# Down projections of four feed-forward blocks computed as seven products of quarters in two passes, with sums of weight quarters made in DRAM by adding transfers

## What is computed

```
u = x @ w_up                       # x: 512 x 1024, w_up and w_gate: 1024 x 2816
g = causal_dwconv(x @ w_gate, ...) # second block: no convolution
down = (silu(g) * u) @ w_down      # w_down: 2816 x 1024
```

## Time and profile before

| | us |
|---|---|
| median of 3 runs (2281.48 to 2284.59) | 2281.77 |
| span of the profiled execution | 2280.9 |
| TensorE busy | 2245.4 (98%) |
| VectorE busy | 1367.0 (60%) |
| ScalarE busy | 1072.6 (47%) |
| GpSimd busy | 737.0 (32%) |
| DMA | mean 98 GB/s |

### The profile page before, as it was taken

One profiled execution on the slowest core, in us unless ns is written; L12 is line 12 of the kernel. 1 busy time (PEld: TensorE's weight loads), 2 busy tenths in 40 slices (PEclk: granted clock), 3 DMA queues, 4 the chain that ended last, 5 costly groups with the idle time before them and its releaser, 6 DMA issues.

```text
span 2280.9 us, 36680 instructions
## 1 busy us (share of the span) xinstructions
PE 2245.4 (98%) x13358; PEld 1934.1 (85%) x13358; DVE 1367.0 (60%) x1963; ACT 1072.6 (47%) x1850; POOL 737.0 (32%) x334
## 2 busy tenths in 40 slices
PE   8999999999999999999999999999999999999998
PEld 6668899988888887899988899988878768999987
DVE  7967666660453436666631899950557963899811
ACT  6665444442555554344432544441535665444512
POOL 6944422244322325321344311144111003311252
PEclk9999999999999999999999999999999999999999
DMA  6632332232211133223332233332422002323332
GB/s 211 197 93 94 110 107 98 99 101 96 80 65 66 64 103 120 96 98 101 102 100 85 93 102 110 95 106 95 149 82 75 29 11 83 107 98 109 101 102 93
DMA packets 64432, 223.79 MB, mean 98 GB/s; under 512 B 7120, under 2 KB 7120, under 8 KB 64336
## 3 DMA queue, kind: packets, MB, share of 16 engines
q1 hardware_dynamic: 60192, 208.30, 27.9%
q10 hardware_dynamic: 4144, 14.16, 2.0%
HBM read 211.88 MB, written 2.10 MB: 94 GB/s over the span
## 4 chain that ended last, share of the span: by engine, by line
PE 86%; DVE 5%; ACT 4%; issue 3%; DMA 1%; POOL 1%; DVEq 0%; SPq 0%; ACTq 0%; POOLq 0%
PE banks L645 9%; PE banks L678 9%; PE banks L680 9%; PE banks L679 9%; PE banks L646 9%; PE banks L647 9%; PE banks L859 5%; PE banks L860 5%; PE banks L861 5%; PE banks L906 3%; PE banks L905 3%; PE banks L904 3%; DVE banks L2603 2%; DMA raw<-ws 1%; PE banks L1257 1%
## 5 line engine op out<-in xcount | busy, mean ns | idle before, releaser
L563 POOL TENSOR_TENSOR wL<-raw,wH 128x1024 fp32r<-128x1024 f32 x194 | 497.6, 2570 | 756.9 <-ACT wH L1457 756.7
L1457 ACT ACTIVATE wH<-raw 128x1024 fp32r<-128x1024 f32 x371 | 391.9, 1058 | 680.8 <-PE banks L680 393.8
L645 PE MATMUL banks<-xH,wH 128*128 128x512 f32 (+1 forms) x1080 | 413.3, 383 | 11.2 <-DVE xL L2135 7.2
L646 PE MATMUL banks<-xL,wH 128*128 128x512 f32 (+1 forms) x1080 | 407.7, 377 | 0.0
L647 PE MATMUL banks<-xH,wL 128*128 128x512 f32 (+1 forms) x1080 | 407.5, 377 | 0.0
L678 PE MATMUL banks<-wH,hH 128*128 128x512 f32 x704 | 273.9, 389 | 0.0
L679 PE MATMUL banks<-wH,hL 128*128 128x512 f32 x704 | 273.9, 389 | 0.0
L680 PE MATMUL banks<-wL,hH 128*128 128x512 f32 x704 | 273.9, 389 | 0.0
L645 PEld LDWEIGHTS banks<-xH,wH 128*128 128x128 f32 x1080 | 203.6, 189 | 56.6 <-DVE wL L2140 7.9
L647 PEld LDWEIGHTS banks<-xH,wL 128*128 128x128 f32 x1080 | 203.6, 189 | 38.1
L646 PEld LDWEIGHTS banks<-xL,wH 128*128 128x128 f32 x1080 | 203.8, 189 | 35.1
(11 more groups left out here) (381 smaller groups left out, 5229.3 us busy)
## 6 DMA issues: line engine op xcount, KB each, us to landing
raw<-ws SPq DMA_DIRECT2D x371, 512.0 KB, 3.3
shifted<-gpad SPq DMA_DIRECT2D x32, 258.0 KB, 4.9
w1b<-w ACTq DMA_DIRECT2D x8, 512.0 KB, 5.6
tmp<-rows ACTq DMA_DIRECT2D x7, 512.0 KB, 3.8
b_row<-rows ACTq DMA_DIRECT2D x5, 512.0 KB, 3.8
tmp<-xT SPq DMA_DIRECT2D x8, 256.0 KB, 6.0
xr<-xN ACTq DMA_DIRECT2D x4, 512.0 KB, 3.7
out<-xr SPq DMA_DIRECT2D x3, 512.0 KB, 2.7
```

Source lines behind the costliest of these rows:

```text
L563: pool.tensor_tensor(wL[:, j, :], raw[:, j, :], fp(wH[:, j, :]), ALU.subtract).then_inc(low_ready, 1)
L645: pe.matmul(bank, wH[:, slot, cols], rh, start=start, stop=False)
L646: pe.matmul(bank, wH[:, slot, cols], rl, start=False, stop=False)
L1457: act.activation(wH[:, c % SLOTS, :], raw[:, c % SLOTS, :], ACT.Copy).then_inc(high_ready, 1)
```

## The change

A down projection is the product of a 512 x 2816 matrix h and a 2816 x 1024 matrix w. The change cuts tokens, hidden channels (11 chunks each) and output columns in halves and computes the four output quarters from seven products of 256 x 1408 by 1408 x 512, in Winograd's arrangement. Each product takes 2 token tiles x 11 chunks x 3 matmuls of 512 columns.

- Pass one makes products 1, 5, 6 and 4 over 11 pairs of chunks, each into 2 banks; ScalarE copies all eight banks into `tmp` (`keep_part`), and GpSimd joins them to three tiles (`down_parts`: fifth - first, sixth - first, first + fourth).
- Pass two makes products 2 and 3, into the banks 4 to 7 of the second half of the tokens (VectorE adds the kept sixth in `seed_banks`), and product 7 into the banks 0 and 2 of the first half. These are completed from the kept tiles: in parts 0 and 1 by adding the kept tiles to the residual ahead (`add_kept`), in parts 2 and 3 by `join_block`, two VectorE operations for each of the two token tiles of the first half, before `post_block` and `update_block` can have them.
- The weights of a down projection now are 39 chunks: 22 chunks of quarters and their sums (DRAM tensor `sums`), 11 plain ones (`X_AT`) and 6 with a third kind of sum (`thirds`, `Y_AT`). GpSimd makes these sums in DRAM with transfers: 14 plain copies of up to 1 MB for each down projection (`copy_base`: for part 0 beside the chunks of the second pointwise projection and the first gate `ple0`, for 1 and 2 beside those of the first attention, for 3 in the second attention), and, beside gate and up, for each of 11 pairs four transfers of 256 KB that add to their destination: the first and the third together, then the second, which waits for the first, and the fourth, which waits for the second. The next pair waits for the fourth and the third.
- The down chunks go through two rings of four slots: the second ring lies where `xH` and `xL` (the parts of x) are, so it can be filled once gate and up are over. Their low parts are VectorE's. The first four chunks of the following stage are all loaded when 36 of the 39 chunks are used up.
- The parts of h are formed pair by pair (`part_sums`, `parts_high`, `part_lows`) in rings of four in `mixXH` and `mixXL`; `hH` and `hL` are gone.
- Semaphores of the row loads are merged to make room for the new ones.

The diff, cut to its core:

```diff
+NP = FT // 2
+X_AT = [FT + 3 * (k // 2) + k % 2 for k in range(9)] + [FT + 15, FT + 16]
+Y_AT = [FT + 3 * (k // 2) + 2 for k in range(8)] + [FT + 13, FT + 13, FT + 14]
...
+DOWN = FT + NP + len(Y_CHUNKS)
...
+            def load_down(inst):
+
+                d0 = CHUNK[f"down{inst}"]
+                for i in range(DOWN):
+                    c = d0 + i
+                    if i < SLOTS:
+                        sp_e.wait_ge(chunk_done, c - SLOTS + 1)
+                    else:
+                        sp_e.wait_ge(chunk_done, max(d0, c - 2 * SLOTS + 1))
+                    to = raw_slot(c)
+                    if i < FT:
+                        sp_e.wait_ge(sum_added, 16 * (3 * (NP * inst + i // 2) + (3 if i % 2 else 1)))
+                        sp_e.dma_start(to, sums[FT * inst + i]).then_inc(loaded(c), 16)
+                    elif i in Y_STARTS:
+                        a, b = Y_CHUNKS[Y_STARTS.index(i)]
+                        w = (b - a + 1) * S
+                        sp_e.wait_ge(third_added, 16 * (NP * inst + b + 1))
+                        sp_e.dma_start(to[:, 0:w], thirds[inst, :, a * S:a * S + w]).then_inc(loaded(c), 16)
+                    else:
+                        sp_e.dma_start(to, ws[c]).then_inc(loaded(c), 16)
+                if inst < 3:
+                    for c in range(d0 + DOWN, d0 + DOWN + SLOTS):
+                        sp_e.wait_ge(chunk_done, d0 + DOWN - SLOTS + 1)
+                        sp_e.dma_start(raw[:, c % SLOTS, :], ws[c]).then_inc(raw_loaded[c % SLOTS], 16)
...
                         low_of_last_sum(u, 1, t)
+                        second_sum(inst, 0, t)
                         low_of_last_sum(u, 2, t)
+                        fourth_sum(inst, 0, t)
+                    first_and_third(inst, SEVENS[inst] - 1)
                     low_of_last_sum(u, 1, SEVENS[inst] - 1)
-                    d0 = CHUNK[f"down{inst}"]
-                    for i in (d0, d0 + 1):
-                        split(i // SLOTS, i % SLOTS)
-                    return d0 + 2
...
+            def copy_base(inst, n):
+
+                d0 = CHUNK[f"down{inst}"]
+                if n < NP:
+                    to, src = FT * inst + 2 * n, d0 + 2 * n
+                    pool.dma_start(sums[to:to + 2].rearrange("c p n -> (c p) n"),
+                                   ws[src:src + 2].rearrange("c p n -> (c p) n")).then_inc(bases_copied, 16)
...
+            def first_and_third(inst, j, t=0):
+
+                c, d = FT * inst + 2 * j, CHUNK[f"down{inst}"] + 2 * j
+                if NP * inst + j:
+                    pool.wait_ge(sum_added, t * 48 + 48 * (NP * inst + j))
+                    pool.wait_ge(third_added, t * 16 + 16 * (NP * inst + j))
+                    pool.sem_inc(adding, 1)
+                pool.dma_start(half_of(sums, t * 2 + c, 1), half_of(ws, t * 2 + d, 0), accum_op=ALU.add).then_inc(sum_added, 16)
+                pool.dma_start(thirds[inst, :, bass.ds(t * S + j * S, S)], half_of(ws, t * 2 + (d + 1), 1), accum_op=ALU.add)\
+                    .then_inc(third_added, 16)
...
+            def second_sum(inst, j, t=0):
+
+                c = FT * inst + 2 * j
+                pool.wait_ge(sum_added, t * 48 + 48 * (NP * inst + j) + 16)
+                pool.sem_inc(adding, 1)
+                pool.dma_start(half_of(sums, t * 2 + (c + 1), 1), half_of(sums, t * 2 + c, 1), accum_op=ALU.add)\
+                    .then_inc(sum_added, 16)
...
-                def h_there(k):
-                    pe.wait_ge(h_ready, FT * inst + k + 1)
-                full_product(f"down{inst}", FT, hH, hL, h_there, banks_free)
+                d0 = CHUNK[f"down{inst}"]
+                lows, parts = DOWN * inst, A_PARTS * inst
+
+                def product(bank, g, n, t, i, half, start=False):
+
+                    a, w = slice(t * P, t * P + P), slice(half * S, half * S + S)
+                    high, low = mixXH[:, g % 4, n, a], mixXL[:, g % 4, n, a]
+                    w_high, w_low = high_slot(d0 + i)[:, w], low_slot_of(d0 + i)[:, w]
+                    pe.matmul(ps[bank], high, w_high, start=start, stop=False, skip_group_check=True)
+                    pe.matmul(ps[bank], low, w_high, start=False, stop=False, skip_group_check=True)
+                    return pe.matmul(ps[bank], high, w_low, start=False, stop=False, skip_group_check=True)
...
+                def second_and_third(k, t, seed=False):
+                    pe.wait_ge(a_low, parts + 3 * NP + 2 * k + 2)
+                    pe.wait_ge(down_low, lows + X_AT[k] + 1)
+                    product(4 + 2 * t, NP + k, 2, t, X_AT[k], 0)
+                    if seed:
+                        pe.wait_ge(seeded, 2 * inst + t + 1)
+                    return product(5 + 2 * t, NP + k, 1, t, X_AT[k], 1)
+
+                def seventh(k, t):
+                    pe.wait_ge(a_low, parts + 3 * NP + 2 * k + 2)
+                    pe.wait_ge(down_low, lows + Y_AT[k] + 1)
+                    return product(2 * t, NP + k, 0, t, Y_AT[k], k % 2)
+
+                pe.sem_inc(low_ready, DOWN)
...
+                    sixth_and_fourth(j).then_inc(chunk_done, 1)
+                first_and_fifth(NP - 2).then_inc(chunk_done, 1)
+                first_and_fifth(NP - 1).then_inc(part_done, 1)
+                sixth_and_fourth(NP - 2).then_inc(chunk_done, 1)
+                sixth_and_fourth(NP - 1).then_inc(chunk_done, 2)
+
+                pe.wait_ge(part_kept, 8 * inst + 4)
+                for k in range(0, NP - 3, 2):
+                    for x in (k, k + 1):
+                        second_and_third(x, 0, seed=x == 4)
+                        second_and_third(x, 1, seed=x == 4).then_inc(chunk_done, 1)
...
+                        pe.wait_ge(part_kept, 8 * inst + 6)
+                    for y in (k, k + 1):
+                        seventh(y, 0)
+                        mm = seventh(y, 1)
+                    mm.then_inc(chunk_done, 1)
+                second_and_third(NP - 3, 0)
+                second_and_third(NP - 3, 1).then_inc(chunk_done, 1)
+                for y in (NP - 3, NP - 2):
+                    seventh(y, 0)
+                    mm = seventh(y, 1)
+                mm.then_inc(chunk_done, 1)
+                seventh(NP - 1, 0).then_inc(block_done, 1)
+                seventh(NP - 1, 1).then_inc(block_done, 1)
+                second_and_third(NP - 2, 0).then_inc(chunk_done, 1)
+                second_and_third(NP - 1, 0).then_inc(block_done, 1)
+                second_and_third(NP - 2, 1)
+                second_and_third(NP - 1, 1).then_inc(chunk_done, 2)
 
...
+                if q < 2 and name != "wout":
+                    act.wait_ge(whole_made, 2 * (2 * int(name == "down3") + q) + 2)
+                elif q < QT - 1:
...
+                def keep_part(to, bank, n):
+                    if n < 4:
+                        act.wait_ge(part_done, 3 * inst + n)
...
-                        low_h(0)
+                        part_sums(0)
+                        low_of_chunk(1)
                     dve.wait_ge(product_done, t * 5 + (5 * u + 5))
                     dve.tensor_tensor(gate, half_bank(4), w, ALU.subtract).then_inc(seven_sum, 1)
                     if inst < 2:
                         older_taps(tmp[:, 1, :], tmp[:, 2, :], f, t, base + 1)
...
+                    if last:
+                        part_lows(0)
...
+                def seed_banks():
+
+                    dve.wait_ge(combined, 3 * inst + 2)
+                    dve.wait_ge(chunk_done, d0 + X_AT[3] + 1)
+                    for t in range(2):
+                        dve.tensor_tensor(ps[5 + 2 * t], ps[5 + 2 * t], kept_sixth[:, t, :], ALU.add).then_inc(seeded, 1)
+
+                def add_kept():
+
+                    dve.wait_ge(combined, 3 * inst + 3)
+                    dve.tensor_tensor(xr[:, 0:2, 0:S], xr[:, 0:2, 0:S], kept_fourth, ALU.add).then_inc(kept_added, 1)
+                    dve.tensor_tensor(xr[:, 0:2, S:D], xr[:, 0:2, S:D], kept_fifth, ALU.add).then_inc(kept_added, 1)
...
+                    def parts(g, chunk):
+                        part_sums(g)
+                        low_of_chunk(chunk)
+                        part_lows(g)
+
+                    for p in range(1, NP):
+                        parts(p, 2 * p)
+                        low_of_chunk(2 * p + 1)
+                    for k in (0, 2, 4, 6):
+                        parts(NP + k, X_AT[k])
+                        parts(NP + k + 1, X_AT[k + 1])
+                        if k == 4:
+                            seed_banks()
...
+                wait_block(name, q)
+                n = 2 * int(name == "down3") + q
+                dve.tensor_tensor(ps[2 * q + 1], ps[2 * q], kept_fifth[:, q, :], ALU.add).then_inc(whole_made, 1)
+                dve.wait_ge(whole_made, 2 * n + 1)
+                dve.tensor_tensor(ps[2 * q], kept_fourth[:, q, :], ps[2 * q], ALU.subtract).then_inc(whole_made, 1)
```

(49 more changed lines are left out.)

346 lines of the change are left out of this document (279 added, 67 removed).

## The result

The changed kernel takes 2328.87 us (median of 4 runs, 2325.07 to 2332.94) where the kernel before took 2281.85 us beside it. The ratio is 1.0203, 95% interval [1.0186, 1.0219]: slower by 2.0%, outside my range of 2238 to 2318; my forecast of 2267 was faster than before.

A forecast was written before the change was run, and what follows sets the result against it. TensorE, busy for 2245.4 of 2280.9 us, was taken as the bound. The terms -59.8 + 7.4 + 17.2 + 1.5 + 19 = -14.7 gave a span of 2266.2, forecast as 2267 us, range 2238 to 2318.

The forecast's parts named there:

- Matmuls removed: Down projections: 462 matmuls where 528 stood in each of four, at 0.2266 us each; -59.8 us.
- VectorE and ScalarE in the down stage: Down stage, steady state: VectorE needs 4.8 us of each 5.44 in pass one, ScalarE less; costed at nothing.
- Rival D: Down stage: VectorE cannot keep up, 18 us on the forecast, 2285 us; chance 0.05.
- Start of down: Start of the down projections: first product waits for low parts of h; +7.4 us (0 to 10).
- End of down: End of the down projections: late chunk loads and copies delay norm work, joins come first; +17.2 us (8 to 22).
- Copies: 14 copies per down projection hold up one load already on the chain; +1.5 us (0 to 4).
- Adding transfers: Gate and up: 176 transfers of 256 KB delay the raw weight loads in flight; +19 us.
- L: Time of an adding transfer from issue to landing, taken as 4.5 us; GpSimd's chain costs nothing below 7.
- d: Delay of a raw load by an adding transfer in gate and up: between nothing and 2.0 us, 0.65 us taken.
- Rival A: Gate and up: loads starve beside adding transfers, 2293 us, or 2336 us if they meet in full; chance 0.22.
- Rival B: Gate and up: GpSimd's row of waits for its own transfers delays TensorE, 2364 us at L = 8; chance 0.10.
- Rival C: Nothing collides, d = 0: 2249 us, down to 2238 with half of the ends hidden; chance 0.18.

The follow-up runs named there:

- e4: Changed kernel with ScalarE's two copies of the following chunks behind the deviations of the first two blocks after down 0, 1 and 2; 2326.86 us.
- e6: Changed kernel with ScalarE's two copies of the following chunks behind the first block's deviation alone after down 0, 1 and 2; 2324.19 us.
- e1: Changed kernel with all 176 adding transfers left out, copies and everything else kept; 2252.57 us.
- e8: As e3, but the 44 adding transfers for down 3 moved to the attention and output projection ahead of gate and up 3; 2291.31 us.
- e9: As e7, and in gate and up 0 and 1 the second and third adding transfers are issued ahead of GpSimd's two long subtractions; 2255.93 us.
- e11: As e9, with the first pair's low parts ahead of VectorE's two taps in gate and up 0 and 1, plus e6's edit; 2249.79 us.
- e2: Changed kernel with the 176 adding transfers made plain ones of the same size at the same places; 2292.38 us.
- e7: As e3, but in gate and up 2 and 3 the two adding transfers are issued after a tile's first product, 3 us earlier; 2265.75 us.
- e3: Changed kernel with the same 176 adding transfers regrouped, first with previous pair's fourth, second with third, each two after a landed load; 2289.23 us.

## Why the prediction was wrong

*Matmuls removed: right.* -59.8 us was predicted; the down stages give -58.8.

*VectorE and ScalarE in the down stage: right.* From 505 to 565 us VectorE is busy for 53.12 of 60 us, 4.82 us in 5.44, with TensorE never idle:

```profile
505.00:565.00 60.00, 60.00 (x267) 49.67 (x266) 53.12 (x82) 42.84 (x68) 6.69 (x4) 1.00 0.68 226
```

Rival D did not occur.

*Start of down: right in size*, 6.7 us where the sum had 7.4. The cure found only 2.3 us in each of two.

*End of down: right in size, in part by luck.* The four stretches cost 3.8, 5.2, 6.0 and 3.1 us (3.7, 5.0, 5.0 and 3.5 in the sum). The step named the late loads, and ScalarE's order behind them. The waits are there: the rows of L900 above are TensorE's first waits behind down 1 and down 2, 5.7 and 5.3 us, where the kernel before has 0.6 and 0.7. But behind each of these two waits the granted clock is at its lower level, which the sum does not have. The first stretch is behind down 2 in the changed kernel, the second in the kernel before:

```profile
1644.00:1649.00 5.00, 5.00 (x25) 4.99 (x24) 2.60 (x4) 3.40 (x11) 0.00 (x0) 0.50 0.02 3
```

```profile
1613.00:1627.00 14.00, 11.79 (x94) 10.64 (x93) 9.46 (x18) 12.49 (x33) 0.00 (x0) 1.00 0.23 77
```

TensorE works at that level for 3.6 us behind down 1 and for 5.8 us behind down 2. A matmul of L900 takes 0.20 us there (22 in 4.31 us), one of its kind 0.13 in the kernel before (16 in 2.05 us); one of 512 columns takes 0.43 at that level and 0.23 above it. So between 0.35 and 0.47 of this time is lost, by estimate 1.3 to 1.7 of the 5.2 us and 2.0 to 2.7 of the 6.0 us. What the late loads cost by themselves is then 3.3 to 4.0 us, less than the 5.0 of the sum. (The kernel before is not at the upper level all the time either: it is at 0.50 from 1797 to 1803 us, and so is the changed kernel from 1827 to 1833.) ScalarE's first deviation begins at 604.86 us, 0.4 us ahead of the last matmul, where it was 5.8. But e4 and e6 show that another order on ScalarE gives little; in e4 GpSimd's low part, which needs ScalarE's copy, came late instead. An earlier load was not tried; the slots of the ring are in use until then.

*Copies: right in kind*, 2.4 us for 1.5, on the one load that the step named.

*Adding transfers: this step failed.* It had +19 us; they cost 76 (e1). L was right: 4.5 us assumed, 4.4 and 4.5 measured for three of the four, 6.5 for the third sum, which has a whole pair's time. GpSimd's chain cost nothing in gate and up: TensorE has no wait for GpSimd there. Wrong was d, the time by which a late load is held up. I took 1.5 us of data, 0.8 us ahead of the load's, which leaves 0.65. The two paired stages lost 21.7 + 22.5 = 44.2 us against e1, 1.30 in each of 34 tiles, and with the 0.16 of slack d is 1.46 us. Both numbers in it were off. The engines are held for 1.84 us, not 1.5. And there was almost no head start. From issue to issue it is even 1.2 us, but GpSimd's transfer needs 1.5 us and more until its data begin (issued at 1418.64, data from 1420.1; in the tile above 1.9 us) and SyncE's load 0.9, so 0.3 to 0.6 us are left. I had taken the two delays as equal, and no row of the kernel before that I read showed either. The 0.8 us themselves were read too short: the load that I put at 1483.4 us is issued at 1483.83.

With 1.84 us and no head start the sum would have had 34 x 1.68 + 19 x 1.16 = 79 us, near the 76 measured. That nearness is luck: it gives the paired stages 57 us, which lost 44, and parts 0 and 1 22 us, which lost 18.1 + 10.8 = 28.9. There the loss is 1.5 us in each of 19 passes, twice the 0.78 that the slack of 0.68 would leave of this d. The sum has one transfer at the late load, as in a paired tile. In a pass of part 0 three are issued around it:

```profile
358.80 0.81 POOL L800 DMA_DIRECT2D sums<-sums  x1 [1.93 <-DMA sums<-sums]
359.99 0.81 POOL L783 DMA_DIRECT2D sums<-ws  x1 [0.37 <-issue]
360.66 0.98 POOL L784 DMA_DIRECT2D thirds<-ws  x1
```

```profile
359.85 4.22 DMA raw<-ws
```

They are the fourth of one pair and the first and third of the next; the late load behind the next three takes 5.02 us. That is the likely cause of the rest, read from this pass and not tested by itself. In gate and up 1 some 1.5 us of the loss are the granted clock, which is at 0.50 from 1042 to 1045 us, behind a wait of 2.1 us.

*Rival A was the case*, between its two prices (2293 and 2336); its condition d > 1.07 was met in the paired loops (1.46). I gave it 0.22 because "DMA is busy for only 32% in this loop". That row is a mean over 20 us. The load with no lead has one place in the tile, and the transfers were issued at that place in each tile, as their order on GpSimd says. *Rival B* was not the case in the changed kernel, but e8 brought it about. *Rival C* would have been 2249 us; e9, in which nothing collides, takes 2256, and e1, which has no adding transfers, 2253. That e11 comes to 2250 is no confirmation, since its starts and ends are shorter than those of the sum.

## What to carry to other kernels

A low mean share of the DMA engines does not say that a transfer added to a loop is free: find the load that has no lead, its 3 us in the loop's period, and where the new transfer's data fall, counting the time from its issue to its data (1.4 us and more here). If it fits, make the place explicit with a wait on an event of the loop; the same 176 transfers cost 76 us in one place and 3 in another. The wait must not stand ahead of work on the same engine for which others wait.

## What was not expected of the hardware

- An adding transfer holds GpSimd for 0.80 to 1.11 us at its issue, a plain one of the same size 0.53 us (e2). The data of an adding one begin 1.3 us or more after the issue starts (1404.67, data from 1406.0), those of a load from SyncE after 0.9.
- With an adding transfer in flight a 512 KB load was stretched from about 3.2 to 5.07 us, while the engines showed as full at under 200 GB/s.
- Behind waits of 2.1, 5.7 and 5.3 us in the changed kernel TensorE's granted clock was at its lower level (0.50) while it worked for 3.5, 3.6 and 5.8 us. By estimate such a wait cost up to 2.7 us beyond its own length.
- Kernels with adding transfers that collide with loads spread by 8 to 20 us from run to run (2282.64 to 2302.97 for e8); those without such collisions, e7 with collisions in parts 0 and 1 alone, and e2 with plain ones by 1 to 6.5 (2248.97 to 2250.13 for e11). These are spreads of 4 runs, 10 for e3 and e8, and why they differ was not tested. Small edits could be told apart only on the latter.
